# Third block of a three-block network: an idle buffer zeroed earlier, pools mixed among their gates, decays of the delta rule moved between matmul tiles

## The chip, the cores and the metric

The kernel runs on one core of one Trainium2 chip. The metric is the device time of one execution in microseconds; lower is better. TensorE does the matrix products, VectorE and ScalarE the elementwise work, GpSimd some of it, and the SyncE queue loads the weights.

## What is computed

The reference applies three transformer-like blocks one after the other to x of 512 tokens by 1024 channels. Only the third is touched. Its mixer projects the normed input h once and builds three branches from slices of the projection, each of which is gated and added to one sum:

```python
kc = nsa_compress(rs(nkc, G), pos_k, phi_k1, phi_k2)      # k and v in overlapping blocks of 32 tokens, plus a position
vc = nsa_compress(rs(nvc, G), pos_v, phi_v1, phi_v2)
y_a = nsa_attention(...)                                   # compressed, selected and window attention, 8 heads
y_b = multiscale_pool(pin, pool_w, pool_scale)             # running means over 2, 4, 8, 16 tokens, minus pin, then 128x128 mixes
y_c = gated_deltanet(dqkv, dz, dbeta, da, dn_conv_w, dn_A_log, dn_dt_bias, dn_norm_g)
g_a, g_b, g_c = jnp.split(jax.nn.sigmoid(mg), 3, axis=-1)
merged = g_a * (y_a @ w_bn) + g_b * (y_b @ w_bp) + g_c * (y_c @ w_bd)
x = x + gt1 * (merged @ w_out)
```

`gated_deltanet` convolves dqkv over four tokens and applies silu, divides each head's q and k by its norm, and runs a delta rule in chunks of 64 tokens. Its decays come from `g = -exp(A_log) * softplus(da + dt_bias)` and the running sums of g within a chunk. They don't depend on the convolution.

## The kernel before

Every matrix product with large weights goes through one scheme. A unit of weights (512 KB, 1024 rows by 128 columns) is loaded into one of four slots of a ring. ScalarE makes its rounded copy `w_high` (L385), VectorE the rest `w_low` (L397, function `vector_ahead`), two units ahead of TensorE at most. TensorE then computes one tile of output in a PSUM bank with 24 matmuls of 128x512 (L421: low by high, high by low, high by high, eight each). A tile of a branch's output projection `y` has 12. Eight PSUM banks go round in turn (`b.bank`); a bank is waited for until it is emptied, and one taken with `hold` is left out of the turn until `drop`.

Each engine has its own instruction stream, written out in the order of stages. At a stage's end ScalarE, VectorE and GpSimd wait until all engines have done the stage (`seal`, `sealed`); TensorE doesn't, it waits only for its operands. The stages that matter, in order:

- down2: the end of block 2. TensorE's last matmul ends at 2764 us.
- qkv3: projection of block 3. `gpsimd_qkv3` loads constants, zeroes buffers (the last is `k3_blocks`) and loads the positions. `vector_qkv3` copies tile m = 0 into `k3_in`; `vector_blocks` (L2779) adds the positions into `k3_blocks` in four instructions; only then comes `w_low` of the next unit. k3_blocks held the place of earlier data of block 2's end.
- nsa: attention in 120 units, in rounds; the outputs of five units gather in one held bank ("no").
- the gates and y tiles of the attention's branch, then pools (`tensor_pools` and its partners): first two rows of gate factors by matmuls with diagonal matrices (L2994, `m_diag` made at L3030). Then four times: a tile of `pin`, VectorE's running sums of it (L3045 to L3051, last operation makes `p_c` or `p_b`), and `mix(q)` (L3004, a single-precision matmul with `p_w`, which the trace counts as two). Then the pools' branch: in two halves, four gate tiles (ScalarE's sigmoid) and four y tiles, each gated by VectorE (L1008) and added to `m_merged` by GpSimd (L1015).
- conv3: twelve tiles. ScalarE copies a tile, VectorE convolves it (L3125, L3128), ScalarE applies silu, TensorE transposes (L3082), and VectorE copies it to `d_qkv` (L3115).
- decay3: a stage of its own. A softplus of 128x16 values in a dozen VectorE instructions (L1029 to L1046) with ScalarE's exponential and logarithm, `d_g` (L3192), transposes (L3150), scans to the running sums `d_gi` (L3205), transposes back (L3157), spread over 128 partitions by four single-precision matmuls of K = 4 (L3163, two each in the trace) with VectorE's copies to `d_gb`, two exponentials. Last come the norms: four times squares (L3224) and sums (L3226) of 128x1024 on VectorE, a root, a reciprocal.
- delta: the delta rule. Its first instructions scale q and k in d_qkv by the norms (L3363, L3364); TensorE's first transposes wait for them (L3256).

## Time and profile before

| | |
|---|---|
| median of 3 runs | 4015.15 us (4011.73 to 4017.32) |
| profiled execution | 4012.13 us, of which the span of the profile is 4010.9 |
| TensorE busy | 3636.6 us, 91% of the span, mean granted clock 0.951 |
| VectorE, ScalarE, GpSimd busy | 51%, 35%, 9% |
| chain that ended last | TensorE 22% of the span, VectorE 4%, ScalarE 1%, GpSimd 1% |

The times of the trace are those of the profiled execution. In it, TensorE's granted clock is given as a share of full speed: 1.00 is 2.4 GHz and 0.50 is 1.2 GHz. An idle time stands in brackets before an instruction's row in a timeline, with what ended it. The names lose the digit 3 in the trace: `k3_blocks` is `k_blocks` there.

### The profile page before, as it was taken

To read this page: it belongs to the slowest core of one execution; us is meant where nothing else is said; L and a number is where in the kernel's file an instruction comes from. 1 tells how busy PE (TensorE), PEld (TensorE's weight loads), DVE (VectorE), ACT (ScalarE), POOL (GpSimd) and SP (SyncE) were. 2 spreads that over 40 slices of the span, in tenths; PEclk is the share of its full clock that TensorE was granted. 3 is DMA by queue.
4 is the path that set the end of the run, shared out by engine and by line. 5 is a ranking of instruction groups with operands and counts; after the bars stand their busy time and mean duration, and the time that the engine had idled before them with its cause. 6 is when DMAs were issued, how large, how long until landed. Compare 5 with 4: busy or idle time off the path is not lost. (4 is left out here: it accounts for less than half of the span.)

```text
span 4010.9 us, 44274 instructions
## 1 busy us (share of the span) xinstructions
PE 3636.6 (91%) x17148; PEld 2948.9 (74%) x17148; DVE 2052.6 (51%) x3285; ACT 1399.0 (35%) x2413; POOL 374.5 (9%) x358
## 2 busy tenths in 40 slices
PE   8999899989998999899897889997897968898999
PEld 7877777877777887767675678786775757777877
DVE  4556375777436226522333466664465376453256
ACT  2224243322423224353223353353352222343244
POOL 1000000043001000021010100000000103112101
PEclk9999999989999999899898899998999979998999
DMA  6455212201223224301221322253201210132355
GB/s 230 174 178 179 86 38 69 81 27 53 85 95 137 95 95 163 115 32 58 79 75 42 95 95 90 97 182 113 72 22 40 84 49 1 43 111 84 95 168 168
DMA packets 106126, 380.16 MB, mean 95 GB/s; under 512 B 11760, under 2 KB 14592, under 8 KB 105792
## 3 DMA queue, kind: packets, MB, share of 16 engines
q1 hardware_dynamic: 100944, 364.86, 27.6%
q0 software_dynamic: 2896, 10.38, 0.8%
q8 instruction: 138, 2.26, 0.2%
q10 hardware_dynamic: 2080, 2.10, 0.2%
q14 instruction: 68, 0.56, 0.0%
HBM read 375.19 MB, written 2.10 MB: 94 GB/s over the span
## 5 line engine op out<-in xcount | busy, mean ns | idle before, releaser
L397 DVE TENSOR_TENSOR w_low<-ring,w_high 128x1024 fp32r<-128x1024 f32 (+1 forms) x637 | 815.0, 1281 | 1087.9 <-ACT w_high L385 1067.1
L421 PE MATMUL bank<-x_low,w_high 128*128 128x512 f32 (+1 forms) x2560 | 1005.5, 396 | 97.7 <-DVE w_low L397 57.2
L421 PE MATMUL bank<-x_high,w_low 128*128 128x512 f32 (+1 forms) x2560 | 992.2, 391 | 0.0
L385 ACT ACTIVATE w_high<-ring 128x1024 fp32r<-128x1024 f32 (+1 forms) x637 | 670.2, 1053 | 914.0 <-PE bank L421 388.0
L421 PEld LDWEIGHTS bank<-x_low,w_high 128*128 128x128 f32 x2560 | 500.4, 195 | 205.5 <-issue 64.3
L421 PE MATMUL bank<-x_high,w_high 128*128 128x512 f32 (+1 forms) x2560 | 630.1, 386 | 0.0
L421 PEld LDWEIGHTS bank<-x_high,w_low 128*128 128x128 f32 x2560 | 500.7, 196 | 101.9 <-issue 2.5
L421 PEld LDWEIGHTS bank<-x_high,w_high 128*128 128x128 f32 x2560 | 467.8, 192 | 100.8 <-issue 1.9
L481 PE MATMUL bank<-w_low,x_high 128*128 128x512 f32 (+3 forms) x416 | 156.6, 376 | 1.3 <-ACT z_z L1636 1.3
L483 PE MATMUL bank<-w_high,x_high 128*128 128x512 f32 (+3 forms) x416 | 155.9, 375 | 0.0
L482 PE MATMUL bank<-w_high,x_low 128*128 128x512 f32 (+3 forms) x416 | 155.3, 373 | 0.0
L567 PE MATMUL bank<-w_low,f3d_in 128*128 128x512 f32 x256 | 101.2, 395 | 2.1 <-DVE f3d_in L538 2.1
L568 PE MATMUL bank<-w_high,f3d_in 128*128 128x512 f32 x256 | 101.5, 397 | 0.0
L569 PE MATMUL bank<-w_high,f3d_in 128*128 128x512 f32 x256 | 101.3, 396 | 0.0
L481 PEld LDWEIGHTS bank<-w_low,x_high 128*128 128x128 f32 x416 | 80.9, 195 | 18.8 <-ACT z_z L1636 2.2
L482 PEld LDWEIGHTS bank<-w_high,x_low 128*128 128x128 f32 x416 | 81.0, 195 | 14.6 <-issue 0.2
L483 PEld LDWEIGHTS bank<-w_high,x_high 128*128 128x128 f32 x416 | 80.8, 194 | 14.3
L839 DVE TENSOR_TENSOR f_hid<-bank,f_gate 128x512 f32<-128x512 f32 x44 | 30.5, 692 | 110.2 <-PE bank L421 110.2
L825 ACT ACTIVATE f_gate<-bank 128x512 f32<-128x512 f32 x44 | 26.3, 598 | 173.2 <-PE bank L421 173.2
L567 PE MATMUL bank<-w_low,o_in 128*128 128x512 f32 x192 | 76.8, 400 | 9.2 <-DVE w_low L397 3.7
L730 POOL TENSOR_TENSOR X<-X,f_norm 128x1024 f32<-128x1024 f32 x6 | 14.3, 2391 | 732.9 <-DVE X L713 636.2
L569 PE MATMUL bank<-w_high,o_in 128*128 128x512 f32 x192 | 76.0, 396 | 0.0
(615 smaller groups left out, 5750.0 us busy)
## 6 DMA issues: line engine op xcount, KB each, us to landing
...
```

The lines of the kernel that those rows point to most:

```text
L385: ac.activation(b.UH[i % NU][:, 0:src.shape[1]], src, ACT.Copy).then_inc(*b.split.act.up("high", i))
L397: dv.tensor_tensor(b.UL[i % NU][:, 0:n], src, b.UH[i % NU][:, 0:n].bitcast(F32), SUB).then_inc(*b.split.dve.up("low", i))
L421: i = pe.matmul(out, w[:, k, c], v, start=n == 0 and q == 0, stop=last and q == 3 * K - 1)
L481: pe.matmul(out, xh, wl[:, q, :], start=k + q == 0, stop=False)
L482: pe.matmul(out, xl, wh[:, q, :], start=False, stop=False)
L483: i = pe.matmul(out, xh, wh[:, q, :], start=False, stop=k + q == 7)
L567: pe.matmul(out, u[:, 0, s], wl[:, 0, c], start=k == 0, stop=False)
L568: pe.matmul(out, u[:, 1, s], wh[:, 0, c], start=False, stop=False)
L569: x = pe.matmul(out, u[:, 0, s], wh[:, 0, c], start=False, stop=k == d.nk - 1)
L730: b.nc.gpsimd.tensor_tensor(x, x, G[:, 1, :], ADD).then_inc(*g.pool.up("normed", t))
L825: ac.activation(s.gate[j % 3], b.bk[s.tag, m], ACT.Silu).then_inc(*g.act.up("silu", j))
L839: dv.tensor_tensor(s.hid[:, j, :], b.bk[s.tag, m], s.gate[j % 3], MUL).then_inc(*g.dve.up("hid", j))
```

## The change

Five things, all in block 3:

1. `k3_blocks` and `k3_pos` lie behind everything that the end of block 2 uses, and a new `gpsimd_blocks` zeroes and loads them on GpSimd during down2. VectorE's first copy no longer waits for zeroing; `vector_blocks` waits for the new signal.
2. In nsa, a "no" bank is dropped two units later, so that the turn of banks skips it for longer.
3. In pools, `mix(q)` stands one tile later, after `pin` tile q+1. The first half's gate tiles come ahead of the branch, with the last mix and the two gate rows between them.
4. The decays are computed during the pools' branch: `between(m)` is called after y tile m on each of TensorE, ScalarE and VectorE. Their buffers and the three small loads on GpSimd move with them. The stage decay3 is gone.
5. The norms belong to conv3: GpSimd squares d_qkv (in two buffers), VectorE sums at m = 9, 10, 11 and after the last tile, and the root follows in the same stage.

```diff
+        behind = Area(b, max(b.c2_end, a.at))
+        self.kp = behind.take("k3_blocks", 2, 32, 62)
+        self.pos = behind.take("k3_pos", 2, 32)
...
+def gpsimd_blocks(b, s):
+    gp = b.nc.gpsimd
+    gp.memset(s.kp, 0.0).then_inc(*s.gk.pool.up("zero"))
+    for i, n in enumerate(("pos_k_3", "pos_v_3")):
+        for h in range(2):
+            gp.dma_start(s.pos[64 * h:64 * h + 64, i, :], b.io[n]).then_inc(b.load_sem(f"{n}{h}"), 16)
...
-        if m == 0:
+        if m == 6:
             dv.wait_ge(*g.pool.at("zero"))
...
-            if not br:
+            if i % 5 == 1 and i > 5:
+                b.drop(("no", i // 5 - 1))
+            if i == N - 1:
                 b.drop(("no", i // 5))
...
         tensor_tile(b, g, ("pin", q), [("pin", q)], 0, b.x, bank.ap)
-        mix(q)
-    tensor_branch(b, s.bp, [g.dve.at("out", 3)])
+        if q:
+            mix(q - 1)
+    tensor_gates(b, s.bp, 0, 1)
+    mix(3)
+    for v in range(2):
+        tensor_gate_row(b, s, v)
+        tensor_gates(b, s.bp, v + 1, v + 2)
+    tensor_gates(b, s.bp, 3, 4)
+    tensor_branch(b, s.bp, [g.dve.at("out", 3)], lambda m: tensor_decay3(b, s, m))
...
+def tensor_decay3(b, s, m):
+    pe, g = b.nc.tensor, s.gg
+    if m == 1:
...
+        pe.wait_ge(*g.dve.at("g"))
...
+    if m == 3:
...
+        pe.wait_ge(*g.dve.at("cum"))
...
+    def norm_sum(c):
+        dv.wait_ge(*g.pool.at("square", c))
+        dv.tensor_reduce(s.RK[:, c, :], s.sq[c % 2], AX.X, ADD).then_inc(*f.up("sum", c))
...
         turn(m - 1)
+        if m >= 9:
+            norm_sum(m - 9)
     turn(11)
+    norm_sum(3)
...
+    for c in range(4):
+        qk = s.QKV[:, c, 0:1024]
+        gp.wait_ge(*s.gcv.dve.at("turned", 7))
+        if c >= 2:
+            gp.wait_ge(*s.gcv.dve.at("sum", c - 2))
+        gp.tensor_tensor(s.sq[c % 2].rearrange("p h d -> p (h d)"), qk, qk, MUL).then_inc(*f.up("square", c))
```

How instructions stand now is shown at three places. The first is TensorE where the pools begin; the row of `a_yh` ends the attention's branch. Before:

```order
L421 MATMUL bank<-a_yh_289,w_high_58 128x512 x4
L2994 MATMUL bank<-m_diag_299,const_53 128x512 [waits s_gated3_vector,s_pools_vector]
L2994 MATMUL bank<-m_diag_299,const_53 128x512 [waits s_gated3_vector]
L2994 MATMUL bank<-m_diag_300,const_53 128x512 [waits s_gated3_vector,s_pools_vector]
L2994 MATMUL bank<-m_diag_300,const_53 128x512 [waits s_gated3_vector]
L421 MATMUL bank<-x_low_57,w_high_59 128x512 [waits s_split_vector,s_gated3_vector]
```

Now the gate rows stand behind the last pin tile, a gate tile and the last mix (`p_b` by `p_w`), and a whole tile follows each pair:

```order
L420 MATMUL bank<-x_high_56,w_high_60 128x512 x8
L3026 MATMUL bank<-p_b_314,p_w_310 128x512 [waits s_pools_vector,s_ld_pool_w_3,s_pools_scalar]
L3012 MATMUL bank<-m_diag_308,const_53 128x512 [waits s_pools_scalar,s_pools_vector]
L3012 MATMUL bank<-m_diag_308,const_53 128x512 [waits s_pools_vector]
L420 MATMUL bank<-x_low_57,w_high_58 128x512 [waits s_split_vector,s_pools_scalar]
L420 MATMUL bank<-x_high_56,w_low_61 128x512
```

The mixes and gate rows have moved from between waits to behind 24 matmuls of other work each. The second place is VectorE at the end of the convolutions, the last two tiles. Before, the decays (`d_g`, `d_sp`) followed on the last copy to `d_qkv`:

```order
L3125 TENSOR_SCALAR c_y_332<-c_in_329,cols_54 128x512 [waits s_conv3_scalar]
L3128 SCALAR_TENSOR_TENSOR c_y_332<-c_in_329,cols_54,c_y_332 128x512 [waits s_conv3_vector] x3
L3115 COPY d_qkv_316<-bank 128x4x128 [waits s_conv3_banks]
L397 TENSOR_TENSOR w_low_61<-ring_49,w_high_58 128x1024 [waits s_split_scalar]
L3125 TENSOR_SCALAR c_y_333<-c_in_330,cols_54 128x512 [waits s_conv3_scalar]
L3128 SCALAR_TENSOR_TENSOR c_y_333<-c_in_330,cols_54,c_y_333 128x512 [waits s_conv3_vector] x3
L3115 COPY d_qkv_316<-bank 128x4x128 [waits s_conv3_banks] x2
L3188 TENSOR_TENSOR d_g_320<-m_ba_264,d_dtb_318 128x16 [waits s_conv3_pool,s_conv3_vector,s_ld_dn,s_conv3_scalar,s_conv3_banks]
L1029 TENSOR_SCALAR d_sp_339<-d_sp_337 128x16 [waits s_decay3_scalar]
L1031 RECIPROCAL d_sp_339<-d_sp_339 128x16 [waits s_decay3_vector]
```

Now the sums over `d_sq`, which wait for GpSimd (`s_conv3_pool`), stand between the tiles, and the root is next:

```order
L396 TENSOR_TENSOR w_low_61<-ring_49,w_high_58 128x1024 [waits s_split_scalar]
L3269 TENSOR_SCALAR c_y_340<-c_in_337,cols_54 128x512 [waits s_conv3_scalar]
L3272 SCALAR_TENSOR_TENSOR c_y_340<-c_in_337,cols_54,c_y_340 128x512 [waits s_conv3_vector] x3
L3255 COPY d_qkv_332<-bank 128x4x128 [waits s_conv3_banks]
L3260 TENSOR_REDUCE d_rk_306<-d_sq_344 128x8 [waits s_conv3_pool]
L3255 COPY d_qkv_332<-bank 128x4x128 [waits s_conv3_banks]
L3260 TENSOR_REDUCE d_rk_306<-d_sq_345 128x8 [waits s_conv3_pool]
L616 TENSOR_SCALAR d_rk_306<-d_rk_306 128x32 [waits s_conv3_vector]
L3282 RECIPROCAL d_rk_306<-d_rk_306 128x32 [waits s_conv3_scalar]
L3284 TENSOR_SCALAR d_rk_306<-d_rk_306 128x4x4 [waits s_conv3_vector]
L3428 TENSOR_TENSOR d_qkv_332<-d_qkv_332,d_rk_306 128x256 [waits s_conv3_pool,s_conv3_vector,s_decay3_vector,s_conv3_scalar,s_conv3_banks]
```

The softplus has gone from here, the sums have come in, and the squares are no longer VectorE's. They stand on GpSimd, whose rows of this stage were, before:

```order
L3139 MEMSET c_in_328 128x3
L3139 MEMSET c_in_329 128x3
L3139 MEMSET c_in_330 128x3
L3140 MEMSET d_state_326 128x512
L3470 MEMSET d_vn_362 128x512 [waits s_decay3_vector,s_conv3_pool,s_decay3_scalar,s_decay3_banks]
```

and are now:

```order
L3290 MEMSET c_in_337 128x3
L3291 MEMSET d_state_334 128x512
L3297 TENSOR_TENSOR d_sq_344<-d_qkv_332 128x1024 [waits s_conv3_vector]
L3297 TENSOR_TENSOR d_sq_345<-d_qkv_332 128x1024 [waits s_conv3_vector]
L3297 TENSOR_TENSOR d_sq_344<-d_qkv_332 128x1024 [waits s_conv3_vector]
L3297 TENSOR_TENSOR d_sq_345<-d_qkv_332 128x1024 [waits s_conv3_vector]
L3536 MEMSET d_vn_363 128x512 [waits s_conv3_vector,s_conv3_pool,s_conv3_scalar,s_conv3_banks]
```

Four products of 128x1024 stand there now, between the memsets of this stage and that of the delta stage (`d_vn`). The third place is VectorE behind the first y tile of the pools' branch (`bp_part` is its gated result), now:

```order
L1012 TENSOR_TENSOR bp_part_323<-bank,bp_gate_319 128x512 [waits s_gated3_scalar,s_gated3_banks]
L3167 TENSOR_TENSOR d_g_302<-m_ba_264,d_dtb_300 128x16 [waits s_ld_dn]
L1035 TENSOR_SCALAR d_sp_327<-d_sp_325 128x16 [waits s_decay3_scalar]
L1037 RECIPROCAL d_sp_327<-d_sp_327 128x16 [waits s_decay3_vector]
L1039 TENSOR_TENSOR d_sp_326<-d_sp_325,d_sp_327 128x16 [waits s_decay3_vector]
L1041 TENSOR_TENSOR d_sp_327<-d_sp_326 128x16 [waits s_decay3_vector]
L1043 TENSOR_SCALAR d_sp_325<-d_sp_327 128x16 [waits s_decay3_vector]
L1046 SCALAR_TENSOR_TENSOR d_sp_325<-d_sp_325,d_sp_327 128x16 [waits s_decay3_vector] x6
L1048 SCALAR_TENSOR_TENSOR d_sp_325<-d_sp_325,d_sp_326 128x16 [waits s_decay3_vector]
L1050 TENSOR_SCALAR d_g_302<-d_g_302 128x16 [waits s_decay3_vector]
L1052 SCALAR_TENSOR_TENSOR d_g_302<-d_sp_325,d_g_302 128x16 [waits s_decay3_vector]
L3171 SCALAR_TENSOR_TENSOR d_g_302<-d_g_302,d_alog_299 128x16 [waits s_decay3_scalar,s_decay3_vector]
```

The softplus of the decays stands between the gated results of tiles 0 and 1 (the next row is `bp_part` again); before, those two followed on each other. On TensorE the first transposes of the decays (`d_g`) stand behind y tile 1:

```order
L420 MATMUL bank<-p_yh_317,w_high_58 128x512 x4
L3127 MATMUL bank<-const_53,d_g_302 4x128 [waits s_decay3_vector,s_pools_vector]
L3127 MATMUL bank<-const_53,d_g_302 4x128 x3
L420 MATMUL bank<-p_yl_318,w_high_59 128x512 [waits s_split_vector,s_gated3_scalar]
L420 MATMUL bank<-p_yh_317,w_low_62 128x512
```

## Rows read from the trace of the kernel before

**Rows 1.** View by windows; its first line names the columns.

```profile
core 0: us, PE busy (x) PEld busy (x) DVE busy (x) ACT busy (x) POOL busy (x), PEclk, DMA share, GB/s
...
2764.00:2779.10 15.10, 0.00 (x0) 0.00 (x1) 5.79 (x7) 3.43 (x4) 8.35 (x10) 0.65 0.28 96
...
3062.40:3144.00 81.60, 63.09 (x208) 44.13 (x209) 31.84 (x45) 11.87 (x15) 0.93 (x7) 0.83 0.17 53
3144.00:3188.50 44.50, 44.50 (x194) 36.31 (x193) 16.64 (x15) 10.94 (x13) 9.03 (x7) 1.00 0.31 93
...
3266.00:3298.60 32.60, 8.60 (x16) 3.29 (x16) 20.70 (x46) 5.58 (x14) 0.01 (x1) 0.50 0.00 0
```

**Rows 2.** TensorE's waits, 2846 to 3039 us: total, times, longest.

```profile
PE bank L2873 <- DVE a_yl L2909: 8.7, 6, 3.4
```

**Rows 3.** TensorE's timeline, first matmuls of two tiles in qkv3.

```profile
2779.13 0.76 PE L421 MATMUL bank<-x_low,w_high 128*128 128x512 f32 x1 [15.16 <-DVE w_low L397]
...
2786.13 0.40 PE L421 MATMUL bank<-x_low,w_high 128*128 128x512 f32 x1
```

**Rows 4.** VectorE's timeline at the start of qkv3: start, duration, operation, idle before.

```profile
2770.72 0.69 DVE L2794 COPY k_in<-bank 128x512 f32<-128x512 f32 x1 [18.17 <-POOL k_blocks L2829]
2773.94 3.78 DVE L2779 TENSOR_TENSOR k_blocks<-k_in,k_pos 64x496 f32<-64x496 f32 x4 [2.53 <-DMA k_pos<-in_pos_v]
```

**Rows 5.** VectorE's timeline, one period of the convolution stage.

```profile
3241.44 1.23 DVE L397 TENSOR_TENSOR w_low<-ring,w_high 128x1024 fp32r<-128x1024 f32 x1 [1.05 <-ACT w_high L385]
3243.04 0.49 DVE L3125 TENSOR_SCALAR c_y<-c_in,cols 128x512 f32<-128x512 f32 x1 [0.37 <-ACT c_in L3101]
```

**Rows 6.** TensorE's timeline, first matmuls of two tiles of the pools' gates.

```profile
3127.37 0.40 PE L421 MATMUL bank<-x_low,w_high 128*128 128x512 f32 x1
...
3132.98 0.40 PE L421 MATMUL bank<-x_low,w_high 128*128 128x512 f32 x1
```

**Rows 7.** TensorE's timeline, pools' mix (two of its four) and decays' spread.

```profile
3094.09 1.10 PE L3004 MATMUL bank<-p_b,p_w 128*128 128x512 f32 x2 [3.23 <-DVE p_b L3051]
...
3104.78 2.04 PE L3004 MATMUL bank<-p_c,p_w 128*128 128x512 f32 x2 [3.96 <-DVE p_c L3051]
...
3278.29 7.17 PE L3163 MATMUL bank<-d_gi,const 4*128 4x512 f32 x8
```

**Rows 8.** TensorE's waits, 3062 to 3300 us, same columns.

```profile
PE bank L3256 <- DVE d_qkv L3364: 13.9, 1, 13.9
PE bank L3004 <- DVE p_b L3051: 7.9, 2, 4.7
PE bank L3150 <- DVE d_g L3192: 7.6, 1, 7.6
PE bank L3004 <- DVE p_c L3051: 6.5, 2, 4.0
...
PE bank L3157 <- DVE d_gi L3205: 3.3, 1, 3.3
```

**Rows 9.** VectorE's timeline in the decay stage.

```profile
3270.24 0.17 DVE L1029 TENSOR_SCALAR d_sp<-d_sp 128x16 f32<-128x16 f32 x1 [3.20 <-ACT d_sp L1054]
...
3273.25 0.18 DVE L3192 SCALAR_TENSOR_TENSOR d_g<-d_g,d_alog 128x16 f32<-128x16 f32 x1
...
3288.54 1.22 DVE L3226 TENSOR_REDUCE d_rk<-d_sq 128x8 f32<-128x1024 f32 x1
...
3298.57 0.42 DVE L3363 TENSOR_TENSOR d_qkv<-d_qkv,d_rk 128x256 f32<-128x256 f32 x1 [0.19 <-DVE d_rk L3232]
```

**Rows 10.** GpSimd's timeline in the pools' branch.

```profile
3150.64 1.31 POOL L1015 TENSOR_TENSOR m_merged<-m_merged,bp_part 128x512 f32<-128x512 f32 x1 [1.43 <-DVE bp_part L1008]
```

**Rows 11.** VectorE's timeline of the same stretch as rows 10.

```profile
3151.03 1.99 DVE L397 TENSOR_TENSOR w_low<-ring,w_high 128x1024 fp32r<-128x1024 f32 x1 [0.47 <-ACT w_high L385]
```

**Rows 12.** Groups of instructions on GpSimd over the span.

```profile
L1576 POOL TENSOR_TENSOR s_lh<-const,m_da 128x1024 f32<-128x1024 f32 x16 | 33.8, 2111 | 172.7 <-ACT m_e L1501 172.7
...
L730 POOL TENSOR_TENSOR X<-X,f_norm 128x1024 f32<-128x1024 f32 x6 | 14.3, 2391 | 732.9 <-DVE X L713 636.2 <-DVE small L707 96.7
```

More of the change, by code:

```diff
@@ L924, in tensor_gates, with tensor_branch @@
         tensor_tile(b, s.g, (s.tag, "g", m), [(s.tag, "g", m)], 0, b.x, bank.ap)
-def tensor_branch(b, s, after):
+def tensor_branch(b, s, after, between=None):
     pe = b.nc.tensor
@@ L938, in tensor_branch @@
         tensor_tile(b, s.g, (s.tag, "y", m), units, j, s.y, bank.ap)
+        if between:
+            between(m)
 def scalar_gates(b, s, m0, m1):
@@ L988, in scalar_branch @@
             scalar_ahead(b, u)
+        if between:
+            between(m)
 def vector_gates(b, s, m0, m1):
@@ L3051, in vector_pools @@
         dv.tensor_tensor(dst[:, 16:32], dst[:, 16:32], x[:, 16:32], SUB).then_inc(*f.up("pooled", q))
-        dv.wait_ge(*g.pe.at("out", q))
-        dv.tensor_scalar(s.YBH[:, q, :], b.bk["pout", q], b.col("pool_scale_3", q), None, MUL).then_inc(*f.up("high", q))
-        dv.wait_ge(*f.at("high", q))
-        dv.scalar_tensor_tensor(s.YBL[:, q, :], b.bk["pout", q], b.col("pool_scale_3", q), s.YBH[:, q, :].bitcast(F32),
-                                MUL, SUB).then_inc(*f.up("out", q))
-    vector_branch(b, s.bp)
+        if q:
+            vector_pool_out(b, s, q - 1)
+    vector_gates(b, s.bp, 0, 1)
+    for v in range(2):
+        vector_gate_row(b, s, v)
+        if v == 0:
+            vector_pool_out(b, s, 3)
+        vector_gates(b, s.bp, v + 1, v + 2)
+    vector_gates(b, s.bp, 3, 4)
+    vector_branch(b, s.bp, lambda m: vector_decay3(b, s, m))
 def gpsimd_pools(b, s):
@@ L3065, in gpsimd_pools @@
     gpsimd_branch(b, s.bp)
+def tensor_decay3(b, s, m):
+    pe, g = b.nc.tensor, s.gg
+    if m == 1:
+        bank = b.bank("gd3", g.dve.at("rows"))
+        for e in bank.emptied:
+            pe.wait_ge(*e)
+        pe.wait_ge(*g.dve.at("g"))
+        for c in range(4):
+            x = pe.transpose(bank.ap[0:4, c * 128:(c + 1) * 128], s.GD[:, c, :], b.ident)
+        x.then_inc(*g.pe.up("rows"))
+    if m == 3:
+        bank = b.bank("eg3", g.dve.at("columns"))
+        for e in bank.emptied:
+            pe.wait_ge(*e)
+        pe.wait_ge(*g.dve.at("cum"))
+        for c in range(4):
+            x = pe.transpose(bank.ap[:, c * 4:c * 4 + 4], s.gi[:, c * 128:(c + 1) * 128], b.ident[0:4, 0:4])
+        x.then_inc(*g.pe.up("columns"))
+        for h in range(4):
+            bank = b.bank(("gb3", h), g.dve.at("spread", h))
+            for e in bank.emptied:
+                pe.wait_ge(*e)
+            pe.matmul(bank.ap, b.const("pick")[0:4, h * 128:(h + 1) * 128], s.gi, start=True,
+                      stop=True).then_inc(*g.pe.up("spread", h))
@@ new lines, in scalar_decay3 @@
+def scalar_decay3(b, s, m):
+    ac, g, f = b.nc.scalar, s.gg, s.gg.act
+    if m == 0:
+        ac.activation(s.BE, s.BA[:, :, 0:4], ACT.Sigmoid).then_inc(*f.up("beta"))
+        ac.wait_ge(*b.arrived("dn_A_log_3"))
+        ac.activation(s.al, s.al, ACT.Exp).then_inc(*f.up("a"))
+        ac.wait_ge(*g.dve.at("a"))
+        scalar_softplus(b, f, "g", s.GD, s.sp[0])
+    if m == 6:
+        ac.wait_ge(*g.dve.at("spread", 3))
+        ac.activation(s.EG[:, :, 0, :], s.EG[:, :, 1, :], ACT.Exp).then_inc(*f.up())
+        gl = s.GB.rearrange("p h (c i s) -> p h c i s", c=4, i=2)
+        for h in range(4):
+            ac.activation(s.EG[:, :, 2:4, h], gl[:, h, :, :, 63], ACT.Exp).then_inc(*f.up())
+        ac.wait_ge(*g.dve.at("rest"))
+        ac.activation(s.tmp2, s.tmp2, ACT.Exp).then_inc(*f.up("to_end"))
@@ L4296, in gpsimd_program @@
     gpsimd_ffn2_down(b, p.c2)
+    gpsimd_blocks(b, m3)
     b.seal("down2", "pool")
@@ L4310, in gpsimd_program @@
     b.seal("conv3", "pool")
-    b.seal("decay3", "pool")
-    for w in b.sealed("decay3"):
+    for w in b.sealed("conv3"):
         gp.wait_ge(*w)
```

244 lines of the change are left out of this document (104 added, 140 removed).

## The prediction

> **What bounds the kernel now.** The page comes first: TensorE is busy 91% of the span, and of what it waits for nothing is large. A change of order can only win where TensorE waits or runs at a lower clock, so I read next the view by windows over block 3's first 750 us, for stretches where TensorE's busy time is well below the length. There are three [rows 1]: 15.1 us without TensorE at the start of qkv3, 81.6 us of pools with 63.1 us busy at clock 0.83, and 32.6 us of decays with 8.6 us busy at 0.50. These are the places of the edits. A fourth, attention, has one wait that bears on them [rows 2]. Then the waits of TensorE and the timelines of the engine that it waits for. The reader is to see in each row in brackets who comes last: nearly always VectorE, in chains of dependent small instructions. I add up the five edits, each against the profiled execution of 4012.1 us (span 4010.9 and 1.2 around it); the median of the runs shown is 3.0 us above that execution.
>
> **A, blocks' buffer.** TensorE ends at 2764.0 and starts at 2779.13 [rows 1, 3]. VectorE stands idle 18.17 us behind the zeroing of k_blocks, then copies in 0.69, waits 2.53 for the positions' DMA, adds in 3.78 [rows 4] and makes `w_low` in 1.23 (as in [rows 5]). That zeroing stood behind a constant's load and four other memsets in GpSimd's stream. With zeroing and positions done in down2, where GpSimd was idle, VectorE's chain is 2764.05 + 0.69 + 3.78 + 1.23 and steps between, 2769.9. TensorE gains 9.2 us; the remaining 6 us stay, since the adding still stands ahead of `w_low`. The first tile then takes 7.00 [rows 3] instead of 5.61 [rows 6], from 1.2 GHz after the idle; were the shorter idle to avoid that, the gain would be 10.6. Should the adding still wait some for another thing (constants are loaded in the same queue), 8. Taken: 9.2.
>
> **B, "no" bank.** 8.7 us of waits in six, longest 3.4, at L2873 for `a_yl` [rows 2]: TensorE asks for a bank soon after its last use. Holding the "no" bank two units longer changes which bank is next, and the reader of a bank gets one or two more rounds. But the rounds of attention are set by the loop of VectorE and ScalarE, which TensorE's other waits there name too, so most of what such a wait costs is made up in the next. Bounds 0 and 8.7; I take 2, nearer to nothing, because the waits are spread over six.
>
> **C, pools.** Now 81.6 us from 3062.4 to 3144.0, 18.5 of them idle, and the rest partly at half speed: the mix's pair takes 2.04 at the lower clock, 1.10 at the higher [rows 1, 7]. The waits for `p_b` and `p_c` are 14.4 of the idle time [rows 8]; the rest is behind `m_diag`. After the change every mix has a tile of other work between its `pin` and itself. A tile is 3132.98 - 3127.37 = 5.61 us [rows 6], and the longest wait was 4.7 [rows 8], so a lag of a tile covers it with 0.9 to spare. The stretch becomes eight tiles, 8 x 5.61 = 44.9, eight single-precision matmuls of 128x512 (four mixes, four gate rows) at 0.85 = 6.8 (the decays' four such products take 7.17 at the lower clock [rows 7], some 1.7 each with their last one's tail; half of that), and 1.1 for the first gate row, since `m_diag` is made only when VectorE gets to it: 52.8. Gain 28.8, call it 29. The cover is VectorE's: 31.8 us busy [rows 1] must now fit in 53 instead of 82, which it does at 60%. If it runs late by 1 us a tile, four mixes wait: bound 25. Above, 30 if the gate row does not wait. The queue that loads weights has to deliver eight units in 53 us, 4.2 MB or 79 GB/s; it already moved 93 in the next stretch [rows 1].
>
> **D1, decays between tiles.** This adds to the branch. TensorE has to wait for `d_g` after y tile 1. From y tile 0's end: gating 0.69, a sum 0.18, exponential and logarithm on ScalarE 0.4, the softplus from 3270.24 to 3273.43, 3.2 [rows 9], 4.6 in all with nothing in between; tile 1 hides 2.7 of it, and 1.9 are waited. The table load ahead of the exponential is done while y tile 0 runs. The scans behind y tile 2 are 3.8 by the same reckoning (gating, and the chain that TensorE waited 3.3 for [rows 8]) against 2.7: 1.1 waited. GpSimd merges for 1.3 in each tile [rows 10], and VectorE's `w_low` took 1.99 beside it [rows 11] instead of 1.23; the small operations with two operands in SBUF are likely held as well, so 0.9 and 0.8 are added. That makes 2.8 + 1.9. Then the transposes 0.5, the columns 0.3 (half of what they take in the decay stage at the lower clock), and the spread, 7.17 at the lower clock [rows 7], 3.4 at the higher. Each of the two idles throws TensorE to the lower clock as at 2779.13, where the tile lost 1.4 [rows 3, 6]: 2.5 for both. Sum +11.4. Bounds: 7.2 (1.9 + 1.1 + 0.8 + 3.4: no blocking, no lower clock) and 16 (another merge caught in the way, 1.3, and the spread at 1.2 GHz, 3.4).
>
> **D2, no decay stage, norms in conv3.** VectorE's last copy of conv3 ends 0.7 us into the 32.6 us window of [rows 1], at 3266.7, and the delta rule's first operation starts at 3298.57 [rows 9]: 31.9. What is left behind that copy: a sum over 128x1024 (1.22 [rows 9]), a scaling, the root, a reciprocal, another scaling: 2.5, as from the last sum to L3363 before. If the rest were free, the gain would be 29.4. It isn't quite. In conv3 VectorE is free 1.05 + 0.37 = 1.4 us of each tile's period [rows 5]; three sums of 1.22 fit. The squares are now GpSimd's: its product of the same shape took 2.11 [rows 12], its other product of 128x1024, `X` by `f_norm`, 2.39 [rows 12]. They start when tile 7 has been copied, beside VectorE's `w_low` and convolution steps. [rows 11] and [rows 10] show what that does: `w_low` starts 0.4 us behind GpSimd's start and ends 1.07 us behind its end, so it did not work while GpSimd did. Four squares of 2.1 to 2.4 with VectorE standing are 8.4 to 9.6, and three sums 3.7, against slack in four periods of 5.7: VectorE ends conv3 6.4 to 7.5 later, and TensorE waits for it. The gain is 29.4 - 7 = 22. Bounds: 29.4 (nothing blocks), 16 (each square also waits for VectorE's instruction and VectorE for it, twice the lateness).
>
> The Trainium skill, page "SBUF — State Buffer", section "Who interferes with whom", says that a VectorE instruction with two inputs in SBUF, or a copy or tensor_scalar in a two-port mode, and a GpSimd instruction that reads SBUF lock each other out whole, whoever starts first, while a reduction never contends. By that rule the sums are free of it and the convolution is not, so D2 would be 22; without it 29.4. By that rule, the trace agrees, at 1.99 for `w_low`.
>
> **Sum.** -9.2 - 2 - 29.0 + 11.4 - 22 = -50.8. 4012.1 - 50.8 = 3961.3 for the execution like the profiled one, and 3964 for the median.
>
> **Rivals.**
> - R1, GpSimd's products hide. D2 29.4 instead of 22 (-7.4), D1 at its low bound (-4.2), A 10.2 (-1.0), B 3 (-1.0): -64.4 in all, 3951. For it: VectorE's convolution takes a scalar per partition, `c_in` and `c_y`, and only `w_low` is proven to block. Against it: that step has two inputs in SBUF as `w_low` has.
> - R2, the waits in the branch cost more. D1 16 (+4.6), D2 18 (+4), C 25 (+4), B 0 (+2), A 8 (+1.2): -35.0, 3980. For it: all the estimates of VectorE suppose that it comes to each chain at once, and in D1 and C it is asked for `w_low` in between.
> - R3, the mixing doesn't take the waits away. VectorE now has the gate tiles' `w_low`, `p_yh` and `p_yl` of the last mix ahead of the next sums. If all 14.4 us of waits stay [rows 8], with the lower clock behind them, C is 29 - 14.4 - 4 = 10.6, the total -32.4, 3983. Against it: a margin of 0.9 us, and 60% load.
> - R4, the other side: the clock. If the three new stops in the branch left TensorE at 1.2 GHz, the branch's 44.5 us of tiles [rows 1] and conv3's twelve tiles of 5.61, 67 us, would take twice as long, +112 and so +61, 4076. It decides when over 51 us of work that now goes at 1.00 goes at 0.50. Against it: at 2779.13 the stop of 15 us was followed by a tile of 7.00 and then back to 5.6 [rows 3, 6].
>
> **How the numbers follow.** Chances: forecast 0.59, R1 0.17, R2 0.16, R3 0.04, R4 0.02, anything else 0.02. The forecast case alone is 3957 to 3972. The range takes in R1 and R2: low 3946 (3951 less 5, as for A 10.6, C 30 and B's bound beyond 3), high 3980. A measurement of this kernel tells 0.2%, 8 us, from no change. Faster by more holds in all cases but R4, which has its 0.02 on the slower side, and a remainder of 0.02 in which waits that no row shows eat the gain, counted as same; 0.96 for faster.
>
> **What the profile of the changed kernel would show.** A: TensorE idle 6 us, not 15.2, at the start of qkv3, ended by `w_low`, and VectorE's first copy right at the end of down2. B: fewer waits for `a_yl`. C: no wait for `p_b` or `p_c` and a stretch of 53 us at clock about 1. D1: two waits of some 3 and 2 us between y tiles, for `d_g` and `d_gi`. D2: four GpSimd rows of over 2 us in conv3, steps of VectorE beside them longer by about as much, TensorE waiting 1 to 3 us in the last three tiles, and 10 us from TensorE's last transpose of conv3 to the delta rule's first wait's end. Wrong it would be, above all, if VectorE's convolution steps stay at 0.78 beside the squares (R1), or if the waits between the y tiles are over 4 us (R2).

## The result, and the profile after

The changed kernel takes 3972.72 us (median of 4 runs, 3969.03 to 3975.0), the kernel before 4016.24 in the same comparison. The ratio is 0.9892, with a 95% interval of 0.9875 to 0.9909: 43.5 us less. The profiled executions stand 43.1 us apart, 3969.03 against 4012.13. The forecast was 3964 in a range of 3946 to 3980.

To see where the time went I cut TensorE's timeline at the same instructions in every kernel: the end of down2's last matmul of 128x256, the last matmul on `k_hidden`, the end of the last on `a_yh`, the start of the first on `p_yl`, the end of the last on `p_yh`, the start of the delta rule's first transpose of `d_qkv`, the start of its last product of `d_vn` and `d_aq`, the end. In microseconds, one profiled execution each:

| kernel | ahead | qkv3 | attention and its branch | pools | y tiles of the pools' branch | convolution, decays | delta | rest | span |
|---|---|---|---|---|---|---|---|---|---|
| before | 2763.96 | 74.25 | 224.17 | 81.83 | 44.45 | 110.73 | 154.56 | 556.95 | 4010.9 |
| after | 2765.33 | 66.24 | 222.07 | 52.90 | 60.19 | 85.67 | 157.68 | 557.72 | 3967.8 |
| difference | +1.4 | -8.0 | -2.1 | -28.9 | +15.7 | -25.1 | +3.1 | +0.8 | -43.1 |
| forecast's term | 0 | A -9.2 | B -2 | C -29.0 | D1 +11.4 | D2 -22 | 0 | 0 | -50.8 |

(The gate tiles between the two halves of the y tiles are in that column.) TensorE's waits from 2750 to 3260 us of the changed kernel, in the columns of [rows 2]:

```profile
PE bank L3220 <- ACT c_s L3243: 7.9, 3, 6.6
...
PE bank L420 <- DVE w_low L396: 6.1, 1, 6.1
PE bank L3321 <- DVE d_qkv L3429: 4.0, 1, 4.0
...
PE bank L3127 <- DVE d_g L3171: 2.5, 1, 2.5
PE bank L3135 <- DVE d_gi L3185: 1.7, 1, 1.7
...
PE bank L3012 <- DVE m_diag L3059: 1.0, 1, 1.0
...
PE bank L420 <- DVE a_yl L2928: 0.7, 1, 0.7
```

Of the waits of [rows 8] those for `p_b` and `p_c` are gone, the one for `d_qkv` has fallen from 13.9 to 4.0, those for `d_g` and `d_gi` from 7.6 and 3.3 to 2.5 and 1.7, and `a_yl` is down to 0.7. The wait for `c_s`, the convolution's last step on ScalarE, has grown: 7.9 us in three waits, the longest of 6.6. The kernel before had one, of the same stretch as [rows 8]:

```profile
PE bank L3082 <- ACT c_s L3105: 3.9, 1, 3.9
```

The windows of the stretches (the start of qkv3, pools, y tiles, convolution, the wait at the delta rule), as in [rows 1]:

```profile
2765.30:2771.40 6.10, 0.03 (x1) 0.00 (x0) 5.83 (x7) 3.43 (x4) 3.03 (x5) 0.87 0.67 233
3053.60:3106.50 52.90, 51.94 (x209) 39.07 (x208) 31.31 (x45) 11.90 (x15) 2.48 (x10) 1.00 0.29 84
3106.50:3166.70 60.20, 56.00 (x210) 41.34 (x210) 25.15 (x46) 16.26 (x26) 9.90 (x7) 0.89 0.22 69
3166.70:3248.40 81.70, 73.77 (x337) 58.98 (x335) 63.74 (x77) 28.54 (x38) 12.21 (x9) 0.97 0.25 80
3248.40:3252.40 4.00, 0.02 (x2) 0.01 (x1) 3.35 (x8) 0.32 (x2) 0.53 (x1) 0.50 0.00 0
```

The idle time at the start of qkv3 is 6.1 us instead of 15.1. The pools' 52.9 us are busy for 51.9 of them at full clock, where it was 63.1 of 81.6 at 0.83. The third row is what the forecast had too low: the y tiles with the decays run at a mean clock of 0.89, with only 4.2 of the 60.2 us idle.

### The profile page after: what moved, and what is told of

It is laid out like the page before. It is cut to its first block and busy times, and to the rows that moved or that the text cites. A ratio compares the mean times of both kernels' runs of the same rounds, so it can differ in the third digit from the quotient of the medians.

```text
span 3967.8 us, 44276 instructions
## 1 busy us (share of the span) xinstructions
PE 3631.9 (92%) x17148; PEld 2948.2 (74%) x17148; DVE 2050.7 (52%) x3281; ACT 1398.7 (35%) x2414; POOL 380.9 (10%) x362
## 5 line engine op out<-in xcount | busy, mean ns | idle before, releaser
L482 PEld LDWEIGHTS bank<-w_high,x_high 128*128 128x128 f32 x416 | 80.6, 194 | 14.2
```

The source lines that it names most:

```text
L482: i = pe.matmul(out, xh, wh[:, q, :], start=False, stop=k + q == 7)
```

## The experiments

Each experiment edits the changed kernel, except e10, which edits the kernel before. Most are read by their stretch, since the parts of the program that no edit touches scatter: the part ahead of block 3 took 2758.8 to 2770.3 us in these executions, and the last column of stretches 556.6 to 564.5. A kernel with one execution is read by its stretch alone. This is the same table for them, with the edited stretch in bold:

| kernel | ahead | qkv3 | attention | pools | y tiles | convolution | delta | rest | us |
|---|---|---|---|---|---|---|---|---|---|
| e1, squares on ScalarE | 2764.09 | 66.16 | 222.00 | 52.86 | 60.19 | **82.89** | 154.20 | 563.91 | 3963.3 (4 runs) |
| e2, decays later | 2765.35 | 66.26 | 222.22 | 52.92 | **50.97** | 85.68 | 153.56 | 557.54 | 3955.78 (4) |
| e3, memsets for squares | 2758.76 | 66.21 | 222.07 | 52.91 | 60.11 | **81.85** | 154.33 | 564.46 | 3961.98 (1) |
| e4, w_low first | 2769.97 | **60.45** | 218.84 | 52.92 | 58.70 | 85.67 | 154.30 | 557.85 | 3959.93 (1) |
| e5, A undone | 2766.03 | **74.23** | 218.51 | 52.86 | 58.66 | 85.66 | 154.83 | 557.72 | 3969.7 (1) |
| e6, B undone | 2762.18 | 66.16 | **221.98** | 52.85 | 60.18 | 85.67 | 157.70 | 557.68 | 3965.67 (1) |
| e7, mix at once | 2762.93 | 66.20 | 222.08 | **71.45** | 58.69 | 85.66 | 157.64 | 557.65 | 3983.55 (1) |
| e8, e1 + e2 + e4 | 2763.34 | **60.63** | 218.70 | 52.92 | **50.94** | **82.92** | 154.29 | 558.16 | 3946.0 (5) |
| e12, e8 with squares in a gap | 2767.59 | **60.46** | 218.83 | 52.91 | **50.98** | **81.53** | 154.19 | 556.61 | 3942.44 (4) |
| e9, e8 with B undone | 2769.09 | 60.46 | **224.49** | 52.87 | 50.97 | 82.85 | 154.18 | 563.09 | 3959.21 (1) |
| e10, before with B alone | 2770.31 | 75.95 | **224.33** | 79.66 | 44.46 | 110.97 | 157.44 | 563.98 | 4028.34 (1) |
| e11, only the spread later | 2765.56 | 66.30 | 222.15 | 52.85 | **55.09** | 85.66 | 154.15 | 556.64 | 3959.62 (1) |

**e5: A undone.** GpSimd's zeroing and the positions go back behind its other memsets of qkv3, and VectorE's first copy waits for them.

```diff
     gpsimd_ffn2_down(b, p.c2)
-    gpsimd_blocks(b, m3)
...
     gp.memset(s.VC[:, 64:128], 0.0).then_inc(*f.up("zero"))
+    gpsimd_blocks(b, s)
...
+        if m == 0:
+            dv.wait_ge(*s.gk.pool.at("zero"))
```

> The changed kernel with the zeroing of k_blocks and the load of the positions put back to the end of GpSimd's part of qkv3, and VectorE's first copy waiting for it again, the rest as changed. From down2's last matmul to the end of qkv3's compression 66.2 us in the changed kernel and 74.3 before. Theory A: 74 to 75, TensorE's wait for w_low 15 instead of 6.1; A alone is worth 8. Rival: the place of the buffer or the positions' DMA has a part of its own, and the stretch is under 72.

The stretch is 74.23 us, that of the kernel before to 0.02. The wait is back, in TensorE's timeline:

```profile
2781.18 0.77 PE L420 MATMUL bank<-x_low,w_high 128*128 128x512 f32 x1 [15.15 <-DVE w_low L396]
```

So A is worth 8.0 us, and nothing else in the change touches that stretch.

**e4: w_low ahead of the adding.**

```diff
             dv.tensor_copy(s.kcv[:, m, :], b.bk["q3", m]).then_inc(*g.dve.up("k", m))
+            vector_ahead(b, ("q3", m + 1))
             vector_blocks(b, s, m)
```

> The changed kernel with the next unit's w_low made ahead of the adding into k_blocks, for the first two tiles of qkv3. In the changed kernel TensorE waits 6.1 us there for w_low, and VectorE adds for 3.8 in between. Theory order: w_low starts when w_high is done at 1.05 us after the barrier, and TensorE's wait is 2.3 to 2.6 us; total 3.5 to 4.5 less. Rival: the wait stays over 5 us, for then it is the barrier and ScalarE's w_high that set it. Rival moved wait: the matmuls over k_blocks come so early that they wait for the adding, 2 us or more at line 2701 of the kernel before's place.

qkv3 takes 60.45 us, 5.8 less, more than the 3.5 to 4.5 expected. TensorE's timeline, its first matmul after the wait and one of the next:

```profile
2772.48 0.48 PE L420 MATMUL bank<-x_low,w_high 128*128 128x512 f32 x1 [2.50 <-DVE w_low L396]
...
2773.02 0.40 PE L420 MATMUL bank<-x_low,w_high 128*128 128x512 f32 x1
```

The wait is 2.5 us, as expected, and so 3.6 shorter. The other 2.2 us, which the expectation left out, are clock: matmuls of 0.40 us stand right behind the wait, where the changed kernel had eleven slow ones (below). No wait at the matmuls over `k_blocks` appeared.

**e6, e9, e10: the held bank.** e6 and e9 take the late drop out again, of the changed kernel and of e8; e10 puts it alone into the kernel before.

```diff
-            if i % 5 == 1 and i > 5:
-                b.drop(("no", i // 5 - 1))
-            if i == N - 1:
+            if not br:
                 b.drop(("no", i // 5))
```

> The changed kernel with the held bank of attention dropped after its last use as before. From the end of qkv3 to the end of the attention's branch: 222.1 us in the changed kernel, 224.2 before. Theory: the waits for a_yl were mostly made up for by other waits, so the stretch goes back by 2, to 224 to 224.5, with waits of about 8.7 us for a_yl in place of 0.7. Rival: it stays at 222 and the difference was the state of the clock; or it gets over 226.

> e8 with the held bank of attention dropped after its last use as in the kernel before. Attention took 218.5 to 218.8 us in three runs with the bank held longer, 222.0 to 222.2 in five, with one stretch of 5 us at clock 0.53 more, and 222.0 in the one run with B undone. If B does nothing, attention takes one of these values again, 218 to 222.5; if it is worth its waits for a_yl, over 223.

> The kernel before with nothing but the held bank dropped two units later. The kernel before took 224.2 us from the end of qkv3 to the end of the attention's branch, with 8.7 us of waits for a_yl. Theory nothing: those waits disappear and others grow, and the stretch takes 218.5 to 224.5 by the clock. Rival: it falls clearly below what any run took, under 217, for the start of the stretch differs there.

e6's waits of TensorE in attention, two of their rows:

```profile
PE bank L2890 <- DVE a_yl L2926: 8.6, 5, 3.6
PE bank L2872 <- ACT a_pt L2984: 7.0, 13, 1.1
```

and e10's:

```profile
PE bank L2855 <- ACT a_pt L2969: 9.4, 15, 1.2
PE bank L2875 <- DVE a_s L2940: 8.2, 8, 2.3
```

(L2872 and L2855 are the same statement.) With the bank held short the 8.6 us for `a_yl` come back, and the waits for `a_pt`, 9.4 with it held long, are 7.0. All of TensorE's waits of the stretch add up to 26.0 to 27.2 us with the short hold (three executions) and 24.2 to 25.3 with the long one (eleven). The stretch took 221.98, 224.17 and 224.49 us with the short hold, and with the long one 218.5 to 218.8 in four executions, 222.0 to 222.2 in six, and 224.33 in one. The waits differ by less than these times do; the rest is clock. The same instructions, some 40 us into attention, in the changed kernel and in e5 (windows, as in [rows 1]):

```profile
2871.00:2876.00 5.00, 5.00 (x20) 3.96 (x19) 2.22 (x10) 1.37 (x8) 0.00 (x0) 0.53 0.02 8
```

```profile
2879.70:2884.70 5.00, 5.00 (x30) 4.39 (x29) 3.55 (x19) 2.55 (x12) 0.00 (x0) 1.00 0.01 3
```

In five microseconds the first did 20 matmuls at clock 0.53, the second 30 at 1.00. Both have places of lower clock in the first 80 us of the stretch, the changed kernel more of them; together they make the 3.5 us between 218.5 and 222.1.

By the expectations, e6's 222.0 is the rival's (B does nothing), e9's 224.49 beside 218.7 and 218.8 is "worth its waits", and e10's 224.33 is "nothing". But e10's value hides a difference. Up to the first matmul of the attention's branch, e10 took 198.7 us and the kernel before 201.2. Then both waited 0.71 us for `a_yl`, and the branch behind it took 25.5 us in e10 and 22.7 or 22.8 in each of the other thirteen. The branch's first 5 us in the kernel before, then in e10:

```profile
3039.58:3044.58 5.00, 5.00 (x21) 4.07 (x22) 0.00 (x0) 5.00 (x9) 0.00 (x0) 1.00 0.00 0
```

```profile
3045.13:3050.13 5.00, 5.00 (x12) 3.98 (x13) 0.00 (x0) 5.00 (x9) 0.00 (x0) 0.50 0.00 0
```

So e10 gained 2.5 us where the bank is held and lost 2.7 to the clock behind it. Without the branch the short hold took 199.0, 201.2 and 201.5 us, the long one 195.5 to 195.8 in four executions and 198.7 to 199.2 in seven. e9 and e10 speak for B, e6 against it. What B does to the waits is shown: 1.7 to 2.0 us less in all in each of the three pairs that differ in B alone. What it does to the time, through the clock, these runs don't settle.

**e7: the mixes at once.** Each `mix(q)` goes straight behind its `pin` tile again; gate rows and gate tiles stay where the change put them.

```diff
         tensor_tile(b, g, ("pin", q), [("pin", q)], 0, b.x, bank.ap)
-        if q:
-            mix(q - 1)
+        mix(q)
     tensor_gates(b, s.bp, 0, 1)
-    mix(3)
...
-        if q:
-            vector_pool_out(b, s, q - 1)
+        vector_pool_out(b, s, q)
...
-        if v == 0:
-            vector_pool_out(b, s, 3)
```

> The changed kernel with each mix put straight behind its own pin tile again on TensorE, and its result taken by VectorE straight behind, the gate rows left between the gate tiles. From the end of the attention's branch to the first y matmul of the pools' branch: 52.9 us in the changed kernel, 81.8 before. Theory lag: the four waits of 2.5 to 4.7 us come back (14.4 together) and half of the matmuls behind each go at the lower clock, 52.9 + 14.4 + 4 to 8 = 71 to 75; the rest of the 29 is the gate rows' (4.1 of waiting, 3 of lower clock). Rival weave: taking the gate rows out of the start and the gates ahead is what pays; then the stretch stays under 65.

The stretch takes 71.45 us, and the waits of [rows 8] are back to a tenth:

```profile
PE bank L3026 <- DVE p_b L3091: 7.9, 2, 4.7
PE bank L3026 <- DVE p_c L3091: 6.5, 2, 4.0
```

Of the 28.9 us of C, 18.5 are the mixes' lag (14.4 of waiting, 4.1 of lower clock). The other 10.4 are the remainder, put down to the new place of the gate rows and gate tiles; no run moved those back by themselves.

**e2 and e11: where the decays wait.** e2 moves both TensorE steps and the VectorE chains back: the transposes of `d_g` and the scans from behind tiles 1 and 2 to behind tile 3, columns and spread from tile 3 to tile 4. e11 moves columns and spread alone.

```diff
 def tensor_decay3(b, s, m):
-    if m == 1:
+    if m == 3:
...
-    if m == 3:
+    if m == 4:
...
 def vector_decay3(b, s, m):
-    if m == 2:
+    if m == 3:
...
-    if m == 3:
+    if m == 4:
```

> The changed kernel with TensorE's transposes of d_g behind y tile 3 instead of 1, the scans on VectorE there too, and the columns and the spread behind y tile 4 instead of 3, so that a tile or four gate tiles lie between each VectorE chain and the TensorE operation that needs it. Changed kernel: y tiles with decays 60.2 us from the first y matmul to the last, 2.5 and 1.7 of them waiting, spread 6.7. Theory chain: both waits go, the clock stays at its higher level and the spread takes 3.4 instead of 6.7: stretch about 50, total 9 to 11 less. Rival price: the spread takes 6.7 by itself, because TensorE waits for nothing there but its rows are slow (K of 4 rows, single precision), then only 5 to 6 less. Rival moved wait: the copies of the spread on VectorE delay w_low or y5, and waits of 2 to 4 us appear at y tile 5: nothing or 3 less.

> The changed kernel with only the columns and the spread moved behind y tile 4; the transposes of d_g stay behind tile 1 and the scans behind tile 2. It parts the two waits. Theory: the wait for d_g of 2.5 us stays and costs itself and up to 1.5 of lower clock behind it; the wait for d_gi (1.7) goes, and the spread takes 3.7 as in e2 instead of 6.5 to 6.7: y tiles with decays 60.2 - 1.7 - 3.0 = 55.5, or 54 with the clock back early. Rival: most of the 9.2 that e2 gained hangs on the first wait; then over 57.

In the changed kernel TensorE's decays look so:

```profile
3114.76 1.01 PE L3127 MATMUL bank<-const,d_g 128*4 128x128 f32 x4 [2.49 <-DVE d_g L3171]
...
3124.13 0.38 PE L3135 MATMUL bank<-const,d_gi 4*128 4x4 f32 x4 [1.71 <-DVE d_gi L3185]
3124.37 6.73 PE L3141 MATMUL bank<-d_gi,const 4*128 4x512 f32 x8
```

in e2:

```profile
3117.89 0.60 PE L3127 MATMUL bank<-const,d_g 128*4 128x128 f32 x4
...
3143.66 0.41 PE L3135 MATMUL bank<-const,d_gi 4*128 4x4 f32 x4
3143.93 3.67 PE L3141 MATMUL bank<-d_gi,const 4*128 4x512 f32 x8
```

and in e11, transposes and spread:

```profile
3115.08 1.01 PE L3127 MATMUL bank<-const,d_g 128*4 128x128 f32 x4 [2.48 <-DVE d_g L3171]
...
3148.16 3.67 PE L3141 MATMUL bank<-d_gi,const 4*128 4x512 f32 x8
```

The spread takes 6.73 us behind the second wait and 3.67 where there is none, so the rival that its rows are slow by themselves falls. e2's stretch is 9.2 us shorter, e11's 5.1: the second wait costs 1.7 itself and 3.4 of clock, the first 2.5 and 1.6. No new wait appeared at tile 5. (e2's median is 16.9 us below the changed kernel's, more than the expected 9 to 11. In the profiled pair, 13.3 apart, 4.1 of the rest lie in the delta rule, which the edit doesn't touch.)

Two things are less simple than this sum. First, the 1.6 us of clock behind the first wait do not always come. The same wait in e5:

```profile
3119.85 0.60 PE L3130 MATMUL bank<-const,d_g 128*4 128x128 f32 x4 [2.49 <-DVE d_g L3174]
```

Here, in e4 and in e7 the transposes take 0.60 us, not 1.01, the matmuls behind them run at the higher clock, and the stretch takes 58.7 us instead of 60.2. None of the three edits touches this stage. Beside these three, e2 gains 7.7. Second, in e2 too the clock falls, after the spread and without a wait:

```profile
3148.80:3152.20 3.40, 3.40 (x10) 2.63 (x9) 0.28 (x2) 0.16 (x1) 0.00 (x0) 0.51 0.00 0
```

The eight-matmul spread itself ran at 1.00, five matmuls of the next tile followed at 1.00, and then eight at 0.51 cost some 1.5 us. The expectation that the clock stays up holds for the spread, not for what stands behind it.

**e1, e3, e12: who makes the squares.** e1 has ScalarE square, behind its silu of tiles 8 to 10 and before that of tile 11. e3 keeps GpSimd and its waits, but lets it only write: two memsets in place of each product. e12 is e8 with ScalarE's squares behind the copy of tiles 8 to 11.

```diff
+    def square(c):
+        ac.wait_ge(*g.dve.at("turned", 7))
+        if c >= 2:
+            ac.wait_ge(*g.dve.at("sum", c - 2))
+        ac.activation(s.sq[c % 2].rearrange("p h d -> p (h d)"), s.QKV[:, c, 0:1024],
+                      ACT.Square).then_inc(*f.up("square", c))
...
         ac.activation(s.cb[m % 3][:, 3:515], b.bk["x3", m], ACT.Copy).then_inc(*f.up("copied", m))
+        if m >= 8:
+            square(m - 8)
...
-        gp.tensor_tensor(s.sq[c % 2].rearrange("p h d -> p (h d)"), qk, qk, MUL).then_inc(*f.up("square", c))
```

> The changed kernel with the four squares of 128x1024 on ScalarE (activation Square) instead of GpSimd; all else the same. From the first q-k tile's copy to the delta rule the changed kernel took 85.7 us from the end of the pools' branch to TensorE's first matmul of the delta rule. Theory lock: GpSimd's products hold VectorE's w_low and convolution steps back for as long as they run; without them VectorE runs late only by its three sums, which fit, so TensorE's waits for c_s (7.9 us in the changed kernel, longest 6.6) fall to about 1.5 and the stretch to about 79.5, total about 6 us less: 3966 to 3968 for a median of 3972.7. Rival sums: the lateness is that of VectorE's own sums; then moving the squares changes nothing, stretch 85 to 86. Second rival: ScalarE's squares (about 1 us each) delay its w_high and silu as much; stretch 82 to 84.

> The changed kernel with each of GpSimd's four products replaced by two memsets of the same buffer (so it leaves the squares of the norms out); the waits are the same, and GpSimd is busy for about 1.8 us each time but only writes. Theory lock by reads: VectorE's tensor_scalar and w_low beside them keep 0.49 and 1.23 us, TensorE's waits for c_s are about 1.5 to 2 us in all, the stretch from the branch's end to the delta rule 79 to 80.5. Rival, any GpSimd work holds VectorE back: as in the changed kernel, w_low or tensor_scalar of about 2.1 us, stretch 84 to 86. Rival sums: also 84 to 86, but with no VectorE row prolonged.

> The three edits of e8, with ScalarE's squares one place earlier in its stream: behind the copy of tile 8, 9, 10 and 11, where ScalarE stood idle 2.9 us for the convolution, not behind silu, where they delayed w_high and the next copy. Theory: the convolution stretch goes from 82.9 us to the 81.9 of the run with GpSimd only writing, TensorE's wait for c_s from 5.5 to about 4.6; 1 us less than e8 in all, within its scatter. Rival: VectorE's sums are the rest of the 5.5, and it stays.

First the changed kernel, VectorE's timeline in the last tile:

```profile
3240.90 1.23 DVE L396 TENSOR_TENSOR w_low<-ring,w_high 128x1024 fp32r<-128x1024 f32 x1
3242.05 2.12 DVE L3269 TENSOR_SCALAR c_y<-c_in,cols 128x512 f32<-128x512 f32 x1
```

and GpSimd's squares:

```profile
3224.62 4.73 POOL L3297 TENSOR_TENSOR d_sq<-d_qkv 128x1024 f32<-128x1024 f32 x2 [54.96 <-DVE d_qkv L3255]
3233.86 2.76 POOL L3297 TENSOR_TENSOR d_sq<-d_qkv 128x1024 f32<-128x1024 f32 x1 [4.51 <-DVE d_rk L3260]
3241.13 2.75 POOL L3297 TENSOR_TENSOR d_sq<-d_qkv 128x1024 f32<-128x1024 f32 x1 [4.51 <-DVE d_rk L3260]
```

The last square begins at 3241.13, beside a `w_low` that runs its usual 1.23 until 3242.13. It then needs until 3243.88, 1.75 us, and the convolution's first step, 0.49 in [rows 5], takes 2.12: it ends 0.29 behind the square. The square held VectorE for 1.6 us, and VectorE had held the square for 1.0. The first square, which nothing was ahead of, agrees with 1.75 us of work: it begins at 3224.62 and so would end at 3226.37, and this `w_low` ends 1.23 behind that:

```profile
3225.59 2.01 DVE L396 TENSOR_TENSOR w_low<-ring,w_high 128x1024 fp32r<-128x1024 f32 x1 [1.05 <-ACT w_high L384]
```

In all, the squares held one `w_low` for 0.8 us and three first steps of the convolution for 1.6 each. Now e3, VectorE and then GpSimd:

```profile
3231.54 1.23 DVE L396 TENSOR_TENSOR w_low<-ring,w_high 128x1024 fp32r<-128x1024 f32 x1
3232.68 1.29 DVE L3269 TENSOR_SCALAR c_y<-c_in,cols 128x512 f32<-128x512 f32 x1
```

```profile
3231.74 0.95 POOL L3297 MEMSET d_sq<- 128x1024 f32 x1 [4.49 <-DVE d_rk L3260]
3232.75 0.95 POOL L3299 MEMSET d_sq<- 128x1024 f32 x1
```

A memset leaves `w_low` at 1.23, with two inputs in SBUF, but the `TENSOR_SCALAR` beside the second one took 1.29, 0.8 more than alone. The expectation that this step keeps its 0.49 is refuted, and e3 is not quite free of blocking. Its stretch is 81.85 us, 3.8 below the changed kernel but above the expected 79 to 80.5. e1 has 82.89, 2.8 below, where about 79.5 was expected, and one wait for `c_s` of 5.5 where 1.5 was:

```profile
PE bank L3220 <- ACT c_s L3253: 5.5, 1, 5.5
```

That is e1's second rival: ScalarE's squares behind silu delayed its copies, which begin 2.4 us after silu in e1 and 1.5 in e12. Put into ScalarE's idle time they cost less, and e12 has 81.53, 4.1 below:

```profile
PE bank L3221 <- ACT c_s L3254: 4.2, 1, 4.2
PE bank L3326 <- DVE d_qkv L3434: 4.0, 1, 4.0
```

The rival that VectorE's own sums make the lateness falls: all three have the same sums. What is left for `c_s`, 4.2 us, is close to the 3.9 of the kernel before, for the chain behind the last tile (copy, convolution, silu). The expectations of 1.5 to 2 us in e1 and e3 had left that wait out.

**e8: the three together.**

> The three edits of e1, e2 and e4 together on the changed kernel: squares on ScalarE, decays' transposes and spread a tile or more later, w_low ahead of the adding. By the stretches of the single runs against those of the changed kernel: 2.8 less in the convolutions, 9.2 in the y tiles, 5.8 in qkv3, 17.8 in all, so 3955 for a median of 3972.7, with 3948 to 3959 as bounds, the lower one if the delta rule takes 154.3 us as in the four runs before instead of the 157.7 of the changed kernel's profile. Rival: the gains don't add, because attention's stretch or the clock takes some back; 3960 or more.

3946.0 us (5 runs), ratio to before 0.9826 (0.9813 to 0.984), and e12 3942.44, ratio 0.9820 (0.9801 to 0.9839). The edited stretches add as they stood alone: qkv3, the y tiles and the convolution are 17.6 us shorter together, 17.8 expected. The time is below the expected 3955 and below its lower bound of 3948, since attention too was at the shorter of its values, 3.4 us less, beside the delta rule's 3.4 that the bound had allowed for; neither is an effect of these edits that was shown.

## Why the prediction was right, point by point

The time, 3972.7, lies in the range, 8.7 above the forecast. The forecast's mechanism held in four of the five parts; for B only the waits behave as forecast, and its time is not shown. The profiled pair is 7.7 us short of the forecast's 50.8: D1 missed by 4.3 us, A by 1.2, D2 by 3.1 the other way, and 5.3 lie where nothing was changed. That D1 and D2 cancel for the most part is luck.

**A, forecast 9.2, measured 8.0 (e5).** The chain went as worked out. VectorE's timeline:

```profile
2765.37 0.69 DVE L2806 COPY k_in<-bank 128x512 f32<-128x512 f32 x1 [11.48 <-PE bank L420]
2766.19 3.83 DVE L2791 TENSOR_TENSOR k_blocks<-k_in,k_pos 64x496 f32<-64x496 f32 x4
2770.06 1.23 DVE L396 TENSOR_TENSOR w_low<-ring,w_high 128x1024 fp32r<-128x1024 f32 x1
```

TensorE waited 6.1 us. The step that missed is "the first tile then takes 7.00"; in TensorE's timeline it takes longer:

```profile
2771.43 0.76 PE L420 MATMUL bank<-x_low,w_high 128*128 128x512 f32 x1 [6.10 <-DVE w_low L396]
...
2775.83 0.63 PE L420 MATMUL bank<-x_low,w_high 128*128 128x512 f32 x1
...
2776.68 0.39 PE L420 MATMUL bank<-x_low,w_high 128*128 128x512 f32 x1
...
2779.53 0.40 PE L420 MATMUL bank<-x_low,w_high 128*128 128x512 f32 x1
```

The tile from 2771.43 to 2779.53 takes 8.1 us, with eleven matmuls of 0.63 us or more, whose starts are 0.43 apart; at the higher clock they take 0.40 and are 0.23 apart. In the kernel before, after a wait of 15.2 us, there were six. With the shorter idle time the slow stretch was 1.1 us longer, and with a still shorter one (e4, 2.5 us) there was none. That takes the idle time's 9.1 us down to 8.0.

**B, forecast 2, measured 2.1 in the pair of profiles, but not shown as B's.** Undone it gave 222.0 or 224.5, alone 224.3. The reason given for taking a small value, that other waits make up for it, is what the rows show: 8.7 us less for `a_yl`, 1.7 more for `a_pt` and 3.5 more for `a_s`, 2.9 less in all. The clock moves the same stretch by more than that, which the prediction did not reckon with.

**C, forecast 29.0, measured 28.9.** No wait for `p_b` or `p_c`, a first gate row that waits 1.0, clock 1.00. e7 shows the cause of 18.5 us of it; the other 10.4, put down to the place of the gate rows and gate tiles, are a remainder.

**D1, forecast 11.4, measured 15.7, near the upper bound of 16, and 14.2 in e4, e5 and e7.** The waits were 2.5 and 1.7 where 2.8 and 1.9 were expected, so the chain was sized well. The term that failed is the spread, "3.4 at the higher" clock: it stands right behind the second wait and ran at the lower, 6.73. I had priced the lower clock by the tile behind a wait, but not looked at which instructions stand there; the case stood only in the upper bound. e2 shows 3.67 without the wait. By e2 and e11 the two waits cost 9.2 us for 4.2 us of waiting, or 7.7 where the clock stayed up behind the first.

**D2, forecast 22, measured 25.1.** Without blocking the forecast gave 29.4; e12 has 110.73 - 81.53 = 29.2. The blocking costs 4.1 us, not 7. The step that missed is "four squares of 2.1 to 2.4 with VectorE standing". A row of a GpSimd product holds also the time in which GpSimd stands for VectorE: 2.75 in the last one, of which 1.75 is work. Four of 1.6 and the sums of 3.7 against 5.7 of slack would have given 4.4; with the 5.7 us for which the rows show VectorE held, it is 3.7. TensorE's longest wait in the last tiles was 6.6 us, where 1 to 3 was expected; 3.9 of it stood there before.

The sign that the prediction named for R1, steps "at 0.78 beside the squares", was the wrong one: three later steps take 2.33 us in both kernels, as each square was over before they began. What was held was `w_low` and the first step.

The Trainium skill's page "SBUF — State Buffer", section "Who interferes with whom", has both halves of e3: that two inputs in SBUF contend only with a GpSimd instruction that reads, and a tensor_scalar in a two-port mode with any. The rows agree: `w_low` 1.23 beside a memset, `TENSOR_SCALAR` 1.29 instead of 0.49. In which mode that instruction ran, no row shows.

**What the sum left out.** +5.3 us of the profiled pair lie where nothing was changed: 1.4 ahead, 3.1 in the delta rule, 0.8 behind. The delta rule took 153.6 to 154.8 us in ten of the kernels and 157.4 to 157.7 in four, among them the changed kernel and e10, whose delta stage is that of the kernel before. The window from 10 to 15 us into the stage, in the changed kernel and then in e8:

```profile
3262.40:3267.40 5.00, 3.48 (x17) 3.29 (x18) 1.51 (x4) 1.06 (x3) 3.41 (x6) 0.74 0.01 2
```

```profile
3239.45:3244.45 5.00, 3.48 (x29) 3.29 (x29) 2.50 (x7) 1.15 (x3) 3.41 (x6) 1.00 0.00 0
```

Cut at the same instructions, the changed kernel falls 1.6 us behind e8 by then and another 1.7 at 40 to 60 us, and it stays 3.4 behind to the end. The waits are 29.4 and 28.4 us in all, so most of the difference is the clock. Why it fell there in four executions and not in ten stays open.

Of the rivals, R1 (GpSimd's products hide) is refuted by e1, e3 and e12. R2 (waits in the branch cost more) came in part: D1 was near its 16 and A at its 8, but D2, C and B were not at theirs. R3 (the waits stay) is refuted by the changed kernel's waits, R4 (the clock stays low) too: the convolution ran at 0.97.
